# A mixture-of-experts decoder trunk: the gate planes of a token by compare-and-multiply, the low planes by a quotient

## The reference

```python
    v1, i1 = lax.top_k(s1, K)
    v2, i2 = lax.top_k(s2, K)
    cand = (v1[..., :, None] + v2[..., None, :]).reshape(B, S, PEER_HEADS, K * K)
    top_v, top_i = lax.top_k(cand, K)
    e1 = jnp.take_along_axis(i1, top_i // K, axis=-1)
    e2 = jnp.take_along_axis(i2, top_i % K, axis=-1)
    expert = e1 * PEER_NKEYS + e2
    gate = jax.nn.softmax(top_v.astype(jnp.float32), axis=-1).astype(h.dtype)
    ...
        act = jax.nn.gelu(jnp.einsum("td,thkd->thk", xt, expert_u[et]), approximate=False) * gt
        return jnp.einsum("thk,thkd->td", act, expert_v[et])
```

## Time and profile before

| | us |
|---|---|
| median of 3 runs | 3004.49 |
| the profiled execution, its own time | 3004.32 |
| its span, first to last instruction | 3002.6 |
| TensorE busy | 2955.5 |
| VectorE busy | 2583.3 |
| GpSimd busy | 1663.7 |
| ScalarE busy | 1532.5 |

### The profile page before, as it was taken

How to read it: one execution, slowest core, us unless ns; L and a number is a source line. 1 busy time by engine, 2 the same in 40 slices (tenths; PEclk the granted TensorE clock), 3 DMA queues, 4 the chain that set the end, 5 groups by cost and what they waited for, 6 DMA issues and landing times.

```text
span 3002.6 us, 45274 instructions
## 1 busy us (share of the span) xinstructions
PE 2955.5 (98%) x15514; PEld 2623.5 (87%) x15514; DVE 2583.3 (86%) x5067; ACT 1532.5 (51%) x2866; POOL 1663.7 (55%) x1010
## 2 busy tenths in 40 slices
PE   7999999999999999999999999999999999999999
PEld 5788899999999888888787788999999998888887
DVE  6987998898987999998775949998998889888887
ACT  6345335776775333343464743347777763333332
POOL 4434358798776555552255634577888875422221
PEclk9999999999999999999999999999999999999999
DMA  7632246999999999999564522359999999999996
GB/s 272 240 110 101 89 159 216 361 335 387 368 353 386 390 394 391 393 388 381 198 223 154 117 68 85 135 201 331 352 369 372 366 378 387 387 378 370 344 352 230
DMA packets 327201, 863.94 MB, mean 288 GB/s; under 512 B 30480, under 2 KB 151328, under 8 KB 326992
## 3 DMA queue, kind: packets, MB, share of 16 engines
q1 hardware_dynamic: 191936, 438.81, 41.2%
q0 software_dynamic: 78608, 285.58, 25.4%
q10 hardware_dynamic: 56448, 136.86, 12.1%
HBM read 752.69 MB, written 94.90 MB: 282 GB/s over the span
## 4 chain that ended last, share of the span: by engine, by line
PE 65%; DVE 21%; ACT 4%; issue 4%; DMA 3%; POOL 3%; ACTq 0%; DVEq 0%; POOLq 0%; SPq 0%
PE banks L1368 23%; PE gbank L1368 11%; PE banks L1348 5%; PE banks L1349 5%; PE banks L1350 5%; PE banks L1328 3%; PE banks L1330 3%; PE banks L1329 3%; DVE u_rows L2331 2%; POOL w_lo L724 2%; DVE hot L2302 2%; DVE pick L2259 2%; DVE pick L2254 1%; DMA raw<-stream_dram 1%; PE gbank L1727 1%
## 5 line engine op out<-in xcount | busy, mean ns | idle before, releaser
L724 POOL TENSOR_TENSOR w_lo<-raw,w_hi 128x1024 fp32r<-128x1024 f32 x355 | 910.0, 2567 | 485.8 <-ACT w_hi L827 482.3
L827 ACT ACTIVATE w_hi<-raw 128x1024 fp32r<-128x1024 f32 x613 | 646.4, 1055 | 583.8 <-PE banks L1368 328.1
L754 POOL DMA_INDIRECT v_rows<-v_dram,row_of x256 | 369.3, 1443 | 596.2 <-DVE fetched L2345 582.0
L1348 PE MATMUL banks<-h_hi,w_hi 128*128 128x368 f32 x2048 | 675.2, 330 | 0.0
L1349 PE MATMUL banks<-h_lo,w_hi 128*128 128x368 f32 x2048 | 672.9, 329 | 0.0
L1350 PE MATMUL banks<-h_hi,w_lo 128*128 128x368 f32 x2048 | 672.9, 329 | 0.0
L1348 PEld LDWEIGHTS banks<-h_hi,w_hi 128*128 128x128 f32 x2048 | 384.4, 188 | 1.6 <-POOL w_lo L724 0.8
L1349 PEld LDWEIGHTS banks<-h_lo,w_hi 128*128 128x128 f32 x2048 | 384.3, 188 | 0.0
L1350 PEld LDWEIGHTS banks<-h_hi,w_lo 128*128 128x128 f32 x2048 | 384.1, 188 | 0.0
L746 POOL DMA_INDIRECT u_rows<-u_dram,row_of x256 | 257.3, 1005 | 164.1 <-DVE z L2331 127.9
L2345 DVE SCALAR_TENSOR_TENSOR fetched<-v_rows,share,fetched 128x1024 f32<-128x1024 f32 x254 | 326.2, 1284 | 2.9 <-DMA v_rows<-v_dram,row_of 2.5
(11 more groups left out here) (403 smaller groups left out, 5118.1 us busy)
## 6 DMA issues: line engine op xcount, KB each, us to landing
raw<-stream_dram SPq DMA_DIRECT2D x613, 512.0 KB, 6.6
gel_dram<-gel ACTq DMA_DIRECT2D x248, 192.0 KB, 5.6
gin<-gel_dram SPq DMA_DIRECT2D x62, 768.0 KB, 11.0
g_dram<-stage ACTq DMA_DIRECT2D x56, 768.0 KB, 11.2
gates<-g_dram SPq DMA_DIRECT2D x64, 672.0 KB, 7.7
ada_w<-ada_dram ACTq DMA_DIRECT2D x36, 512.0 KB, 7.5
ada_mid<-ada_dram ACTq DMA_DIRECT2D x24, 512.0 KB, 5.0
ada_first<-ada_dram SPq DMA_DIRECT2D x8, 1024.0 KB, 18.4
```

The costliest lines, as they stand in the source:

```text
L724: pool.tensor_tensor(w_lo[:, s, :], raw[:, s, :], w_hi[:, s, :].bitcast(F32), ALU.subtract).then_inc(split_lo, 1)
L754: pool.indirect_dma_start(v_rows[:, j % V_ROWS, :], None, (v0, v1)[layer], bass.IndirectOffsetOnAxis(ap=row_of[:, j:j + 1], axis=0)).then_ ...
L827: act.activation(w_hi[:, s, :], raw[:, s, :], ACT.Copy).then_inc(split_hi, 1)
L1348: pe.matmul(out, wh, h_hi[:, k, 0:DENSE_U], start=(k == 0), stop=False)
```

## The change

VectorE compares only the first key number by the wide instruction (512 columns instead of 1024). The high plane of a token is then made by one tensor_scalar of 128 columns: the key numbers compared with the token's second key number and multiplied by its gate's high part, both per-partition scalars. The second one-hot plane is no longer there, so ScalarE makes the low plane from the high one, with the quotient low / high as its scale, and waits for the high plane where it waited for hot. The quotient is made once ahead of the stage (low_share: a divisor that is high, or 1 where high is 0; subtract; reciprocal; multiply), and once more for the 16 extra columns. gate_hi gets a place of its own in SBUF, and high_part in PSUM is gone.

```diff
@@ -278,6 +278,7 @@
     causal = sb("causal", [P, P])
     rowsel_at = place[0]
     rowsel = sb("rowsel", [LOW_ROW + HEADS, HEADS, P], F32R)
+    iota_at = place[0]
     iota = sb("iota", [P, P])
     mod = sb("mod", [P, 2, ADA])
     adab = sb("adab", [P, 2, ADA])
@@ -419,8 +420,7 @@
     exT = sb("exT", [P, 2, DENSE_T])
     expert = sb("expert", [P, PICKS])
     gate_lo = sb("gate_lo", [P, DENSE_T])
-    hot = sb("hot", [P, 2, 2, QUAD, NKEYS], F32R)
-    gate_hi = hot[:, 0, 0].rearrange("p t e -> p (t e)")[:, 0:DENSE_T]
+    hot = sb("hot", [P, 2, QUAD, NKEYS], F32R)
     place[0] = max(place[0], ranked_end)
     row_of = sb("row_of", [P, PICKS], U32)
     share = sb("share", [P, PICKS])
@@ -434,6 +434,9 @@
     gate_extra = z_extra[:, 0:EXTRA]
     turned_extra = sb("turned_extra", [P, 2 * EXTRA])
     u_end = place[0]
+    place[0] = rowsel_at
+    gate_hi = sb("gate_hi", [P, DENSE_T], F32R)
+    assert place[0] <= iota_at
     place[0] = share_at
     gate_extra_hi = sb("gate_extra_hi", [P, EXTRA], F32R)
     place[0] = u_end
@@ -469,7 +472,6 @@
 
 
     keys_at = bank[2][:, 0:NKEYS]
-    high_part = bank[2][:, NKEYS:]
 
     h_rows = gbank[0][:].rearrange("p t n e -> p (t n e)")
     pair_sums = [b.rearrange("p (t n e) -> p t n e", t=PAIR, n=2) for b in (bank[3], misc[2], misc[3])]
@@ -1121,10 +1123,8 @@
             act.wait_ge(S("ex_tp"), past["ex_tp"] + 3)
             for n in range(2):
                 act.activation(exT[:, n, :], misc[n][:, 0:DENSE_T], ACT.Copy).then_inc(S("exT"), 1)
-            act.activation(gate_hi, misc[2][:, 0:DENSE_T], ACT.Copy).then_inc(S("exT"), 1)
+            act.activation(gate_hi[:], misc[2][:, 0:DENSE_T], ACT.Copy).then_inc(S("exT"), 1)
             act.activation(keys_at, iota[:], ACT.Copy).then_inc(S("exT"), 1)
-            act.wait_ge(S("exT"), past["exT"] + 3)
-            act.activation(high_part, gate_hi.bitcast(F32), ACT.Copy).then_inc(S("exT"), 1)
 
             def low_planes(q):
 
@@ -1132,9 +1132,9 @@
                     act.wait_ge(S("gate_lo"), past["gate_lo"] + 1)
                 if q == EXTRA_QUAD:
                     act.wait_ge(S("extra_by_dve"), past["extra_by_dve"] + GATES_SPLIT)
-                act.wait_ge(S("hot"), past["hot"] + q + 1)
+                act.wait_ge(S("one"), past["one"] + q + 1)
                 for u in range(QUAD):
-                    last = act.activation(plane[:, q % 2, u, 1, :], hot[:, q % 2, 1, u, :].bitcast(F32), ACT.Copy,
+                    last = act.activation(plane[:, q % 2, u, 1, :], plane[:, q % 2, u, 0, :].bitcast(F32), ACT.Copy,
                                           scale=gate_lo[:, QUAD * q + u:QUAD * q + u + 1])
                 last.then_inc(S("one_lo"), 1)
 
@@ -1724,7 +1724,7 @@
                     pe.wait_ge(S("g_out"), past["g_out"] + p - 2)
                 for t in range(PAIR):
                     u = PAIR * (p % 2) + t
-                    last = pe.matmul(pair_sums[p % 3][:, t].rearrange("p n e -> p (n e)"), hot[:, q % 2, 0, u, :],
+                    last = pe.matmul(pair_sums[p % 3][:, t].rearrange("p n e -> p (n e)"), hot[:, q % 2, u, :],
                                      plane[:, q % 2, u].rearrange("p n e -> p (n e)"), start=True, stop=True)
                 last.then_inc(S("g_mm"), 1)
 
@@ -2279,9 +2279,18 @@
             link(dve.scalar_tensor_tensor(out=z[:], in0=extra_ex[0], scalar=float(NKEYS), in1=extra_ex[1],
                                           op0=ALU.mult, op1=ALU.add))
             dve.tensor_copy(expert[:].bitcast(U32), z[:]).then_inc(S("picked"), 1)
-            dve.wait_ge(S("exT"), past["exT"] + 5)
-            dve.tensor_tensor(gate_lo[:], misc[2][:, 0:DENSE_T], gate_hi.bitcast(F32), ALU.subtract
-                              ).then_inc(S("gate_lo"), 1)
+            dve.wait_ge(S("exT"), past["exT"] + 4)
+
+            def low_share(low, high, divisor):
+
+                dve.scalar_tensor_tensor(out=divisor, in0=high, scalar=0.0, in1=high, op0=ALU.is_equal, op1=ALU.add)
+                link(dve.tensor_tensor(low, low, high, ALU.subtract))
+                link(dve.reciprocal(divisor, divisor))
+                return dve.tensor_tensor(low, low, divisor, ALU.mult)
+
+            link(dve.tensor_copy(gate_lo[:], misc[2][:, 0:DENSE_T]))
+            low_share(gate_lo[:], gate_hi[:].bitcast(F32), stage[:, 0, 0:DENSE_T // BATCH, :].rearrange("p e t -> p (e t)")
+                      ).then_inc(S("gate_lo"), 1)
             dve.wait_ge(S("gate_lo"), past["gate_lo"] + 1)
 
             def low(t, off=0):
@@ -2294,19 +2303,18 @@
             def one_hots(q):
 
                 tok = slice(QUAD * q, QUAD * q + QUAD)
-                full = [P, 2, QUAD, NKEYS]
+                full = [P, QUAD, NKEYS]
                 if q >= 2:
                     dve.wait_ge(S("g_mm"), past["g_mm"] + 2 * (q - 1))
                 if q == EXTRA_QUAD:
                     dve.wait_ge(S("extra_by_dve"), past["extra_by_dve"] + GATES_SPLIT)
-                dve.tensor_tensor(hot[:, q % 2], keys_at.unsqueeze(1).unsqueeze(1).to_broadcast(full),
-                                  exT[:, 0:2, tok].unsqueeze(3).to_broadcast(full),
-                                  ALU.is_equal).then_inc(S("hot"), 1)
-                dve.wait_ge(S("hot"), past["hot"] + q + 1)
-                wide = [P, QUAD, NKEYS]
-                dve.tensor_tensor(plane[:, q % 2, :, 0, :], hot[:, q % 2, 1].bitcast(F32),
-                                  high_part[:, tok].unsqueeze(2).to_broadcast(wide), ALU.mult
-                                  ).then_inc(S("one"), 1)
+                dve.tensor_tensor(hot[:, q % 2], keys_at.unsqueeze(1).to_broadcast(full),
+                                  exT[:, 0, tok].unsqueeze(2).to_broadcast(full), ALU.is_equal)
+                for u in range(QUAD):
+                    one = slice(QUAD * q + u, QUAD * q + u + 1)
+                    last = dve.tensor_scalar(plane[:, q % 2, u, 0, :], keys_at, exT[:, 1, one],
+                                             gate_hi[:, one].bitcast(F32), ALU.is_equal, ALU.mult)
+                last.then_inc(S("one"), 1)
 
             def gates_out(p):
 
@@ -2389,9 +2397,10 @@
                     dve.transpose(turned_extra[:], z_extra[:]).then_inc(S("extra_by_dve"), 1)
                 if n == EXTRA_LO:
                     dve.wait_ge(S("extra_by_act"), past["extra_by_act"] + GATES_ROUNDED)
-                    dve.tensor_copy(high_part[:, DENSE_U:], gate_extra_hi[:].bitcast(F32))
-                    dve.tensor_tensor(gate_lo[:, DENSE_U:], gate_extra, gate_extra_hi[:].bitcast(F32), ALU.subtract
-                                      ).then_inc(S("extra_by_dve"), 1)
+                    dve.tensor_copy(gate_hi[:, DENSE_U:], gate_extra_hi[:].bitcast(F32))
+                    link(dve.tensor_copy(gate_lo[:, DENSE_U:], gate_extra[:]))
+                    low_share(gate_lo[:, DENSE_U:], gate_extra_hi[:].bitcast(F32), h_extra[:, 0:EXTRA]
+                              ).then_inc(S("extra_by_dve"), 1)
                 if n >= NKEYS - V_AHEAD:
                     product(n - NKEYS + V_AHEAD)
                     a_low(n - NKEYS + V_AHEAD)
```

More of the change, by code:

```diff
@@ L165 @@
 COUNTS = {"scores": N_WQ, "sc": N_WQ, "ranked": N_WQ, "gate_arg": 1, "gate_exp": 1, "ex": 3, "ex_tp": 3,
-          "exT": 5, "hot": QUADS, "one": QUADS, "one_lo": QUADS, "gate_lo": 1, "g_mm": PAIRS_OF_TOKENS, "g_hi": PAIRS_OF_TOKENS, "g_out": PAIRS_OF_TOKENS, "stored0": 16 * PIECES * ((STORED + 1) // 2), "stored1": 16 * PIECES * (STORED // 2), "picked": 3,
+          "exT": 4, "one": QUADS, "one_lo": QUADS, "gate_lo": 1, "g_mm": PAIRS_OF_TOKENS, "g_hi": PAIRS_OF_TOKENS, "g_out": PAIRS_OF_TOKENS, "stored0": 16 * PIECES * ((STORED + 1) // 2), "stored1": 16 * PIECES * (STORED // 2), "picked": 3,
           "h_rows": 2, "u_row": 16 * U_SUMS // U_ROWS, "extra_in": EXTRA_IN, "extra_moved": EXTRA_OUT, "extra_by_act": 3, "extra_by_dve": 2, "v_row": 16 * PICKS // V_ROWS, "dotted": U_SUMS, "z_gel": 2,
```

## The result

The changed kernel takes **3049.19 us** (median of 4 runs, 3047.28 to 3050.62) beside 3003.76 for the kernel before in the same session: a ratio of 1.0147, 95% interval 1.0135 to 1.0159. It is slower, as forecast, but by 45 us and not by 14: 3049 lies 16 us above the upper end of the range.

What follows compares the result with a forecast made beforehand. TensorE was taken to bound the gate stage, with VectorE as cover. Start 4.6, low-plane loop 2.3 and second split 0.1 us, in each of two layers, made 14.0 us on 3004.3: 3018.3 us, range 3009 to 3033.

Steps and rivals of the forecast that it cites:

- What bounds the kernel: Gate stage: TensorE bounds, VectorE is nearly full but only cover; time taken off it returns at most about 1 us per layer.
- the first stretch: Quads 26 to 50, where low planes close a loop: TensorE waits 2.3 us a layer, 6.2 at 0.315 us per tensor_scalar.
- The wide instructions of a quad: VectorE's work per quad: 1.86 us becomes 1.65 with tensor_scalars 0.26 us apart, 0.21 less, saving nothing by itself.
- the first rival: Tensor_scalars in the gate stage: the second scalar column costs as much as the first, 29 us more, 3033 us; chance 0.2.
- The turn: Loop of compare, low planes, high copy and sum: 4.15 us becomes 4.66, or 4.82 at 0.315, against TensorE's 4.57.
- The second stretch: Quads 74 to 95, without slow dots: 1.9 us behind against 1.95 of lead, so nothing; 3.3 us at 0.315.
- DMA, GpSimd and the rest only shift: All other engines' work in the gate stage: moves in time only, with no cost of its own in the sum.
- The second split: Quotient for 16 extra columns at tile EXTRA_LO: five more small operations, some 0.9 us, against about as much lead; 0.1 us.
- a further lock: One more operation on the 16 extra columns falls behind GpSimd's w_lo in each layer: 2.4 us more, 3023 us; chance 0.1.
- The start: Quotient ahead of TensorE's first pair: 4.6 us a layer, reciprocal 2.54 us; the pair waits first, then h_extra.
- cover that I did not see: Low-plane loop has hidden cover, only the quotient's delay before the first pair stays: 3013.5 us; chance 0.2.
- VectorE as the bound: VectorE sets the gate stage's pace: its saving comes off, at most 40 us, 2964 us; faster by over 0.2%, chance 0.03.

Runs made afterwards that it cites:

- with one column: Changed kernel with the constant 1 in place of the tensor_scalar's second per-partition scalar: 3030.65 us, ratio 1.0104.
- second profile: The changed kernel itself measured and profiled once more, nothing altered: 3048.74 us, ratio 1.0162.
- The run from PSUM: Changed kernel with the operands of the 16-column split in PSUM, one instruction more: 3042.90 us, ratio 1.0131.
- the wait moved alone: Kernel before with one edit, ScalarE's low planes wait for the end of the multiply, not for the compare: 3029.96 us, ratio 1.0096.
- the planes first: Changed kernel with each quad's four tensor_scalars put ahead of its 512-column compare: 3028.03 us, ratio 1.0080.
- two parts, filled: Changed kernel, starting quotient made for 8 tokens first and 376 later, plus 10 unread matmuls before TensorE's wait for h_extra: 3039.15 us, ratio 1.0121.
- all three repairs: Changed kernel with tensor_scalars ahead of the compare, starting quotient in two parts, and the 16-column split's operands in PSUM: 3010.30 us, ratio 1.0026.

## Why the prediction was right in sign and wrong in size

**What bounds the kernel** held: VectorE is cover, 0.2 us less in a quad brought nothing, and a loop longer than TensorE's quad showed in full. Two sums are off in the last digit (a tile is 4.46 by the numbers given, the first stretch at 0.315 is 6.3), and nothing hangs on them.

**The failed step** is the one in "The wide instructions of a quad", where the tensor_scalar with two per-partition scalars was put at the row with one, 0.26 us. It is 0.319, 0.004 over the other bound, and longer by 0.06 itself. I had both ends and took the measured one, though the prediction's own reading of the row gave 0.055 us for a column; the first rival, at 0.2, was the case. The sign of being wrong that was set at more than 0.32 us wasn't even reached, and yet the loop passed 4.82. By that rival's price, 3033, the kernel is still 16 us off, for three reasons:

- *The turn* is 4.90 and not 4.82, since the last tensor_scalar's own length (0.402, not 0.335) stands in the path: 0.61 + 3 × 0.319 + 0.402 + 0.035 = 2.0. Put into the prediction's formula for the first stretch, 18 × 4.90 + 17.1 − 96.0 − 1.6 gives 7.7 us; measured 7.2. That these are close is partly luck. The formula keeps three long turns of 5.5 us, and the changed kernel has none: its 21 turns from quad 26 took 102.8 us, 4.89 each, where the formula has 105.3, and the three turns behind them lost 1.6 us, where 0.5 was put. The second stretch came out at 5.7 against 21 × 0.33 = 6.9 less its lead of 1.95. There "DMA, GpSimd and the rest only shift" failed too: in layer 1 TensorE waited 2.0 us for two late w_lo, and with one column such a wait of 0.8 us is most of the 1.1. So a term was put at zero because lead and loss were nearly equal, and it was no zero.
- *The second split* was put at 0.1 us, and a further lock at 2.4 with a chance of 0.1, which was the case. Measured 4.0 and 5.1 (4.8 and 2.8 in the second profile). Here I counted five small instructions by their fixed times and did not ask of each what it reads. By the earlier trace rows one that reads two SBUF operands had been caught. Of the new ones a cast goes from SBUF to SBUF and the last multiply reads two SBUF operands, and both were caught; the four between them ran while GpSimd was between its two w_lo. The section that the prediction named beside the row (the Trainium skill, SBUF — State Buffer, "Who interferes with whom") also says that an instruction of VectorE with at most one SBUF input and outside the two-port modes does not contend with GpSimd. The run from PSUM agrees, 0.16 to 0.27 us for each of seven. The lower clock behind the wait comes on top: in the one split of the two profiles without it, 2.8 us were lost.
- *The start*, foretold 4.6, measured 5.5 and 4.9: near in its sum, and right in its reciprocal, 2.55 us. The 3.3 us estimated from the Trainium skill (VectorE: DVE Perf Modes, "First, the fixed hardware budget") was too long. The way was another: no wait of 2 us at the turn of h, but TensorE at its lower clock. No term of the sum held the clock. The four stretches of it in the two gate stages last 20.5 us together, so some 10 us of matmul time went to them; a part of that TensorE would have waited anyway.

Of the other rivals, cover that I did not see is refuted by the wait moved alone, and VectorE as the bound by the planes first.

## What to carry to other kernels

Where a wait is moved to a later instruction, work out the loop it closes and compare it with the bounding engine's step, before counting what the instructions save; if the two lie within a tenth, the price of one operand decides, and the range must be taken from the dear end. Put first on an engine what another engine waits for. Behind a long wait look at the granted clock before judging a repair: a gain can be there in the waits and be taken back by the clock, and filling the wait tells which. See in the trace that the filling stands at the wait.

## What the runs showed of the hardware

- A tensor_scalar of 128 columns from PSUM costs 0.26 us from start to start with one per-partition scalar and 0.319 with two; it lasts 0.343 and 0.402.
- TensorE's clock fell to its lower level behind waits of 3.17, of 0.6 and 2.0, and of 1.8 us, and stayed there for 3 to 14 us, in the same kernel differently from one execution to the next. Each such stretch cost 1.7 to 6.8 us. The length of the wait alone didn't decide: behind 2.91 us it fell in one layer of the changed kernel's second profile and stayed up in the other, and it stayed up behind 3.14 us (two parts, filled, second split of layer 2) and behind 1.3 (all three repairs).
- A reciprocal of 384 columns took 2.55 us, of 16 columns 0.25 to 0.27.
- A cast of 16 columns from SBUF to SBUF stood 2.50 us beside GpSimd's subtraction, and a multiply of two SBUF operands 2.82; the same columns by way of PSUM took 0.16 and 0.17, the multiply with one operand in PSUM 0.17.
